# A new order for the end of the third block: high parts of the output projection's input in their own buffer, outputs and variances of the last heads ahead of the last gate tiles

## The reference, cut to what matters

```python
def _mixer_c(h, hg_s, lower_bound, w_in, hg_gn, w_out):
    qp, fp, ip, gp = _split(jnp.einsum('bld,de->ble', h, w_in), C_SPLITS)
    f = lower_bound + (1.0 - lower_bound) * jax.nn.sigmoid(fp)
    q, k, log_f, v = silu(qp), 1.0 - f, jnp.log(f), ip        # 8 heads of 128
    o, s_new = _hgrn2(q, k, log_f, v, hg_s)
    o = _head_norm(o, hg_gn, False) * jax.nn.silu(gp)         # per-head RMS norm, gain, gate
    return jnp.einsum('ble,ed->bld', o, w_out), s_new         # output projection
...
x = x + mix
h = _rmsnorm(x, p['ln_ffn'][l])
logits = h @ w_router + b_router; top-2 softmax; 8 experts of d_ff 2816; y = _rmsnorm(x + moe)
```

## Time and profile before

| | us |
|---|---|
| median of 3 runs | 1553.61 |
| lowest, highest | 1551.95, 1554.43 |
| the profiled execution, in all | 1554.71 |
| its span, first to last instruction | 1552.9 |
| TensorE busy | 1502.3 (97%) |
| VectorE busy | 1172.6 (76%) |
| ScalarE busy | 911.2 (59%) |
| GpSimd busy | 86.6 (6%) |
| HBM traffic over the span | 259 GB/s |

### The profile page before, as it was taken

How to read it: one execution, slowest core, us unless ns; L and a number is a source line. 1 busy time by engine, 2 the same in 40 slices (tenths; PEclk the granted TensorE clock), 3 DMA queues, 4 the chain that set the end, 5 groups by cost and what they waited for, 6 DMA issues and landing times.

```text
span 1552.9 us, 23238 instructions
## 1 busy us (share of the span) xinstructions
PE 1502.3 (97%) x8623; PEld 1326.7 (85%) x8623; DVE 1172.6 (76%) x1290; ACT 911.2 (59%) x907; POOL 86.6 (6%) x92
## 2 busy tenths in 40 slices
PE   7999998999999989998999999999999999999997
PEld 5899788999999989987878888888888888888885
DVE  5756677545456797666688898988989888898886
ACT  4544535443334553333477777868778787777863
POOL 1023100000000000111110000000000000000002
PEclk9999999999999999999999999999999999999999
DMA  8577624996456423433599999999999999999993
GB/s 215 155 135 149 115 86 119 287 295 196 129 149 194 139 72 98 136 119 94 199 400 348 392 366 400 388 357 385 369 392 394 365 384 359 399 378 379 392 356 118
DMA packets 214583, 403.86 MB, mean 260 GB/s; under 512 B 14467, under 2 KB 131503, under 8 KB 214386
## 3 DMA queue, kind: packets, MB, share of 16 engines
q1 hardware_dynamic: 203104, 372.82, 69.1%
q0 software_dynamic: 6208, 22.06, 4.6%
q10 hardware_dynamic: 5202, 8.03, 1.5%
HBM read 372.58 MB, written 30.28 MB: 259 GB/s over the span
## 4 chain that ended last, share of the span: by engine, by line
PE 88%; DVE 8%; issue 1%; ACT 1%; DMA 1%; DVEq 0%; ACTq 0%; SPq 0%
PE bank L485 26%; PE bank L486 25%; PE bank L487 25%; PE bank L688 2%; DVE dense_lo L1726 1%; PE bank L942 1%; PE bank L1089 1%; PE bank L730 1%; PE bank L625 1%; ACT dense_hi L1293 1%; DVE w_lo L2261 1%; PE bank L680 1%; DMA arena<-in_x_sample 1%; PE bank L643 0%; DVE arena L2098 0%
## 5 line engine op out<-in xcount | busy, mean ns | idle before, releaser
L2261 DVE TENSOR_TENSOR w_lo<-arena,w_hi 128x2048 fp32r<-128x2048 f32 (+1 forms) x280 | 597.0, 2165 | 86.3 <-ACT w_hi L1605 85.0
L1605 ACT ACTIVATE w_hi<-arena 128x2048 fp32r<-128x2048 f32 (+1 forms) x280 | 500.6, 1819 | 114.4 <-PE bank L487 112.6
L485 PE MATMUL bank<-w_hi,xg_hi 128*128 128x512 f32 (+1 forms) x768 | 288.1, 375 | 2.8 <-DVE w_lo L2261 2.3
L486 PE MATMUL bank<-w_lo,xg_hi 128*128 128x512 f32 (+1 forms) x768 | 286.7, 373 | 0.0
L487 PE MATMUL bank<-w_hi,xg_lo 128*128 128x512 f32 (+1 forms) x768 | 285.9, 372 | 0.0
L1726 DVE TENSOR_TENSOR dense_lo<-ring,dense_hi 128x2048 fp32r<-128x2048 f32 (+1 forms) x78 | 169.2, 2170 | 121.6 <-ACT dense_hi L1293 121.5
L1293 ACT ACTIVATE dense_hi<-ring 128x2048 fp32r<-128x2048 f32 (+1 forms) x78 | 140.5, 1803 | 160.2 <-PE bank L487 134.3
L485 PE MATMUL bank<-h_hi,dense_hi 128*128 128x320 f32 x512 | 165.6, 324 | 17.2 <-DVE h_lo_o L1738 6.2
L485 PEld LDWEIGHTS bank<-w_hi,xg_hi 128*128 128x128 f32 x768 | 144.9, 189 | 32.0 <-issue 3.5
L487 PEld LDWEIGHTS bank<-w_hi,xg_lo 128*128 128x128 f32 x768 | 144.6, 188 | 26.0
L486 PEld LDWEIGHTS bank<-w_lo,xg_hi 128*128 128x128 f32 x768 | 144.9, 189 | 25.0
(11 more groups left out here) (420 smaller groups left out, 2328.0 us busy)
## 6 DMA issues: line engine op xcount, KB each, us to landing
arena<-in_w_moe_down SPq DMA_DIRECT2D x176, 512.0 KB, 6.5
arena<-in_w_moe_gate SPq DMA_DIRECT2D x128, 512.0 KB, 6.7
arena<-in_w_moe_up SPq DMA_DIRECT2D x128, 512.0 KB, 6.7
arena<-in_w_moe_gate SPq DMA_DIRECT2D x64, 384.0 KB, 5.4
arena<-in_w_moe_up SPq DMA_DIRECT2D x64, 384.0 KB, 3.9
ring<-in_w_in_ab SPq DMA_DIRECT2D x32, 512.0 KB, 9.0
ring<-in_w_in_c SPq DMA_DIRECT2D x32, 512.0 KB, 4.6
expert_rows<-ZERO SPq DMA_DIRECT2D x12, 1024.0 KB, 7.6
```

The source lines that it names most:

```text
L485: mm(out, left[0], right[0], start=start, stop=False)
L486: mm(out, left[0], right[1], start=False, stop=False)
L1605: fn(WH[SLOT_OF[p]][:, 0:unit_size(p)], STAGE[:, s, 0:unit_size(p)], ACT.Copy).then_inc(S("unit_hi"), 1)
L2261: v.tensor_tensor(WL[w][:, 0:n], STAGE[:, s, 0:n], WH[w][:, 0:n].bitcast(F32), ALU.subtract).then_inc(S("unit_split"), 1)
```

## The change

The order behind g4 is rewritten. The outputs of heads 6 and 7, their squares and the second variance group now come before gate tile g7, and g6 after state5 and turn7; state4 comes before the first variance group. The high and low parts of the heads become steps of the list, "h u", on ScalarE and VectorE; the scales of heads 6 and 7 and the second root and reciprocal become ordinary steps too. The silu of the gates is taken in three calls, tiles 0 to 3, 4 and 5, 6 and 7. The high parts go to a buffer of their own, HH_O, at arena word 5120, where the squares lie, so that h u waits for the variance group of its head to be read. One memset moves from before `projected_out` to behind its additions. Number and kind of TensorE's matmuls, and all DMAs, are the same; ScalarE issues one silu call more.

```diff
--- before.py
+++ after.py
@@ -73,9 +73,9 @@
     xend0 kend0 v0 xb0 v1 pb0 wh db1 wh xb1 wl lb0 turn0 lb1 v2 la8 v3 db2 pb1 v4 wl wh xb2 wl out0 v5 v6 pb2
     lb2 db3 state0 turn1 v7 xb3 lb3 sq0 v8 wh pb3 out1 wl v9 turn2 db4 out2 sq1 db5 xb4 lb4 state1 v10 state2
     pb4 db6 xb5 g0 lb5 turn3 sq2 xb6 wh v11 pb5 out3 wh wl pb6 sq3 lb6 wl g1 db7 xb7 g2 pb7 g3 lb7 end1 state3
-    xend1 wh g4 lb8 kend1 g5 wh wl turn4 turn5 silug0 out4 wl sq4 gate0 out5 sq5 varc0 rootc0 state4 g6 gate1
-    gate2 mixc0 g7 gate3 state5 turn6 turn7 out6 mixc1 mixc2 mixc3 out7 state6 wl sq6 gate4 gate5 mixc4 sq7
-    gate6 mixc5 wh silug1 gate7 state7
+    xend1 wh g4 lb8 kend1 wh wl g5 turn4 turn5 silug0 out4 sq4 gate0 out5 sq5 wl gate1 state4 varc0 rootc0
+    turn6 gate2 gate3 state5 turn7 g6 out6 sq6 silug1 mixc0 mixc1 mixc2 mixc3 h0 h1 h2 h3 out7 sq7 gate4 gate5
+    mixc4 mixc5 h4 h5 varc1 rootc1 g7 state6 silug2 gate6 gate7 mixc6 h6 mixc7 h7 wh wl state7
 """.split()]
 
 CONST = {}
@@ -268,6 +268,7 @@
         HH = parts("h_hi", AT_HT, KD, NT)
         HL_A, HL_C, HL_O = parts("h_lo_a", AT_ARENA + 22064, KD, NT), parts("h_lo_c", AT_ARENA + 15616, KD, NT), \
             parts("h_lo_o", AT_ARENA + 20736, KD, NT)
+        HH_O = parts("h_hi_o", AT_ARENA + 5120, KD, NT)
         HH_F, HL_F = parts("h_hi_f", AT_ARENA + 15360, KD, NT), parts("h_lo_f", AT_ARENA + 17920, KD, NT)
         U_F, U_C = region(17920, KD, NT), region(15616, KD, NT)
 
@@ -853,11 +854,10 @@
                 w = need_unit(kind, 0, 0)
                 b = [open_bank("dve", j) for j in range(2)]
                 for n, k in enumerate(order):
-                    if k == HEADS[1][0]:
+                    if kind == "oab" and k == HEADS[1][0]:
                         for u in HEADS[1]:
                             head_scale(heads, u)
-                        if kind == "oab":
-                            n_rows()
+                        n_rows()
                     pe.wait_ge(S(out), n + 1)
                     for j in range(2):
                         ins = product3(b[j][:, 0:NT], [x[:, k, j * P:(j + 1) * P] for x in w], [x[:, k, :] for x in src],
@@ -991,8 +991,7 @@
                     after_empty(pe, (("V", 1, u // 4), u % 4 // 2, 2))
                     state_prompt(1, u)
                     piece_along(state_samples(1, u))
-            head_variances("hn1", 1)
-            projection_out("oc", (HH, HL_O), "hn1")
+            projection_out("oc", (HH_O, HL_O), "hn1")
 
 
             pe.wait_ge(S("router_in"), 32)
@@ -1414,7 +1413,8 @@
 
             def mixed_high(out, src, u):
 
-                fn(HH[:, u, :], src[:, u, :], ACT.Copy).then_inc(S(out + "_hi"), 1)
+                hi = {"mix0": HH, "mix1": HH_O}[out]
+                fn(hi[:, u, :], src[:, u, :], ACT.Copy).then_inc(S(out + "_hi"), 1)
 
             def centered(u):
                 b = take(("cen", u))
@@ -1553,8 +1553,8 @@
                     after_empty(act, ("c", "q", 7))
                     fn(Q[:, 4:8, :], Q[:, 4:8, :], ACT.Silu).then_inc(S("q_silu"), 1)
                 elif name == "silug":
-                    after_empty(act, ("c", "g", 4 * u + 3))
-                    at = slice(4 * u, 4 * u + 4)
+                    at = (slice(0, 4), slice(4, 6), slice(6, 8))[u]
+                    after_empty(act, ("c", "g", at.stop - 1))
                     fn(GC[:, at, :], GC[:, at, :], ACT.Silu).then_inc(S("g_silu"), 1)
                 elif name in ("xa", "xb"):
                     level_exps("ab".index(name[1]), 7 - u)
@@ -1574,14 +1574,12 @@
                     fn(SQH["hn1"][u], OH[:, u, :], ACT.Square).then_inc(S("hn1_squares"), 1)
                 elif name == "rootc":
                     head_roots("hn1", u)
+                elif name == "h":
+                    after_fill(act, ("hn1", "var", 0 if u in HEADS[0] else 1))
+                    after_empty(act, ("hn1", "scale", u))
+                    mixed_high("mix1", OH, u)
                 elif name == "state":
                     prompt_state(1, u)
-            after_fill(act, ("c", "g", 7))
-            for u in range(KD):
-                if u == 2:
-                    head_roots("hn1", 1)
-                after_empty(act, ("hn1", "scale", u))
-                mixed_high("mix1", OH, u)
             projected_out("oc", "n3")
             root("n3")
             b = take(("n3", "rt"))
@@ -1735,7 +1733,8 @@
             def mixed_low(out, src, u, lo, place):
 
                 dve.wait_ge(S(out + "_hi"), place + 1)
-                v.tensor_tensor(lo[:, u, :], src[:, u, :], HH[:, u, :].bitcast(F32), ALU.subtract).then_inc(
+                hi = {"mix0": HH, "mix1": HH_O}[out]
+                v.tensor_tensor(lo[:, u, :], src[:, u, :], hi[:, u, :].bitcast(F32), ALU.subtract).then_inc(
                     S(out + "_h"), 1)
 
             def gained(tag, row, k, dst):
@@ -2003,6 +2002,8 @@
                 if lo is not None:
                     low(tag, KD - 1, dst, lo, hi)
                     add_squares(tag, KD - 1)
+                else:
+                    v.memset(HN[SMP:P, 2, :], 0.0)
                 split_dense()
                 scale_of(tag)
 
@@ -2179,20 +2180,14 @@
                 elif name == "mixc":
                     dve.wait_ge(S("gated1"), u + 1)
                     scaled_head(OH, "hn1", u)
+                elif name == "h":
+                    mixed_low("mix1", OH, u, HL_O, u)
                 elif name == "gate":
                     dve.wait_ge(S("hn1_squares"), u + 1)
-                    dve.wait_ge(S("g_silu"), u // 4 + 1)
+                    dve.wait_ge(S("g_silu"), (1, 1, 1, 1, 2, 2, 3, 3)[u])
                     v.scalar_tensor_tensor(out=OH[:, u, :], in0=OH[:, u, :], scalar=prow("hg_gn", u), in1=GC[:, u, :],
                                            op0=ALU.mult, op1=ALU.mult).then_inc(S("gated1"), 1)
             after_fill(dve, ("lv", 1, 0))
-            for u in range(KD):
-                if u == 2:
-                    head_reciprocals("hn1", 1)
-                if u in HEADS[1]:
-                    dve.wait_ge(S("gated1"), u + 1)
-                    scaled_head(OH, "hn1", u)
-                mixed_low("mix1", OH, u, HL_O, u)
-            v.memset(HN[SMP:P, 2, :], 0.0)
             v.memset(ONE[SMP:P, 2, :], 0.0)
             projected_out("oc", "n3", 8, U_R)
             b = take("logit_rows")
```

## The result

The changed kernel takes 1544.46 us (median of 4 runs, 1543.50 to 1545.08), the kernel before beside it 1553.42 us (4 runs, 1551.95 to 1554.43). The ratio is 0.9944, 95% interval 0.9932 to 0.9956: 8.96 us less. The forecast was 1546.3, which is 7.3 us less than the runs known then.

A forecast was written before the change was run, and what follows sets the result against it. TensorE, 97% busy, was taken as the bound, with the experts hanging on the projection's last tile. Pure work 64.0, low clock 4.4 and waits 0.3 make 68.7 against 76.05 us: 7.3 less, 1546.3 us, range 1542.5 to 1551.5.

The forecast's parts named there:

- Rival 3: The experts' stage absorbs the earlier projection end, so the time stays at 1553.6 us; chance 0.08.
- The gaps, 6.16 us: TensorE's idle times before the output projection and its heads 6 and 7, 4.73 + 1.14 + 0.29 us, all to go.
- The layout by hand: Four engine queues laid out from 678.74 us by measured durations; projection to start at 717.2 instead of 722.02.
- The tight place at the second variances: Second variance group at 707.8 waits for head 7's square on ScalarE, ending at 707.6; 0.2 us spare.
- The other tight place: Third projection tile at 724.3 needs the second weight unit's low part, ending near 724.2; no spare to speak of.
- The table loads: An extra 1.28 us load on ScalarE from splitting the silu, without drain; with drains, some 2 us less gain.
- pure work: TensorE's time from g5's end to behind the projection without gaps or low clock, 64.0 us in both orders.
- the second episode: A second low-clock fall, likely between 703 and 709 us amid outputs, scales and variances without a weight tile: 1.5 us.
- the tight waits: Charge of 0.3 us for the two places with thin spare, bounded by 0 and 1.5 us.
- Rival 1: Third low-clock episode and both tight waits lost, 1.5 us each: gain 4.3 us, 1549.3 us; chance 0.16.
- Rival 4: Clock stays low from 684.6 until 3 us into the projection: 5.3 us slower, 1558.9 us; chance 0.09.
- Rival 2: The clock never falls in the new order: stretch 64.0 + 0.3, gain 11.7 us, 1541.9 us; chance 0.07.

The follow-up runs named there:

- e1: The kernel before, old order, with only the high parts moved to their own buffer HH_O and the memset moved: 1552.15 us, ratio 0.9994.
- e4: The changed kernel with gate tile g6 moved between the outputs of heads 4 and 5: 1544.98 us, ratio 0.9962 to the kernel before.
- e3: The changed kernel with one added TensorE wait before the projection, for the second weight unit's high part: 1551.06 us, ratio 1.0001 to the kernel before.
- e2: The changed kernel with the high parts back in the old shared buffer, so h0 to h5 stand behind g7: 1547.94 us, ratio 0.9968 to the kernel before.
- e6: The changed kernel with the silu of gate tiles 4 to 7 in one call behind g7 again: 1546.23 us, ratio 0.9964 to the kernel before.
- e7: The changed kernel with state4 and g6 between the outputs of heads 4 and 5, and state5 ahead of turn6: 1542.28 us, ratio 0.9921 to before.
- e9: The changed kernel with only state4 between the outputs of heads 4 and 5, and state5 ahead of turn6: 1541.58 us, ratio 0.9930 to before.
- e5: The changed kernel with state6 moved ahead of g7: 1546.34 us, ratio 0.9958 to the kernel before.
- a2: The changed kernel run again, unedited, in a second group on another chip: 1547.22 us, ratio 0.9968 to the kernel before.
- a3: The changed kernel run a third time, unedited, in a third group on another chip: 1545.34 us, ratio 0.9954 to the kernel before.
- e8: The kernel of e7 run again, unedited, on another chip: 1540.54 us, ratio 0.9927 to the kernel before.

## Why the prediction was right, and where it was off

**What bounds the kernel.** Right. TensorE's own gaps and clock set the stretch, and the end of the program moved with the router's product: 798.03 us behind it, 798.11 before, and 796.99, 797.02, 798.42 and 797.47 in e1 to e4, although their moments lie between 742.8 and 756.4. Rival 3, the shift not carried, is out. What is left of the spread goes with the clock behind the product: over all thirteen profiles it is 796.9 to 797.0 us where the clock never falls there, 797.5 to 798.7 with 6.8 us at 0.50 and 799.4 to 799.9 with 10.2. One reading of the earlier trace rows was too wide: the DMA engines are nearly free from 745 to 755, but their share is 1.09 in the slice from 684. Nothing in the forecast hung on it.

**The gaps, 6.16 us.** Right: all three are gone. e3 shows that they carried most of the gain, as a gap of 4.68 us put back brought 6.64 of the 9.73 us back on the stretch.

**The layout by hand.** It held to within 0.7 us against turn4, which starts 0.21 us later: scales from 701.61 (forecast 701.7), second variances at 707.69 (707.8), scale 6 at 714.08 (714.4), projection at 716.87 (717.2). The tight place at the second variances is visible on ScalarE. Its timeline after:

```profile
702.26 0.47 ACT L1574 ACTIVATE arena<-arena 128x320 f32<-128x320 f32 x1
702.75 1.28 ACT L1558 ACT_TABLE_LOAD   x1
704.04 0.74 ACT L1558 ACTIVATE arena<-arena 128x640 f32<-128x640 f32 x1
704.69 1.53 ACT L1417 ACTIVATE h_hi_o<-arena 128x320 fp32r<-128x320 f32 x4
...
707.08 0.47 ACT L1574 ACTIVATE arena<-arena 128x320 f32<-128x320 f32 x1
```

Head 7's square ends at 707.55 and the variances start at 707.69: 0.14 us spare where I had counted 0.2. The other tight place is VectorE's last split:

```profile
721.61 2.29 DVE L1724 TENSOR_TENSOR dense_lo<-ring,dense_hi 128x2048 fp32r<-128x2048 f32 x1 [1.31 <-ACT dense_hi L1292]
```

It ends at 723.90, and the third tile starts at 724.01 (forecast 724.2 and 724.3). Neither wait shows, so the 0.3 us that I charged were not due. Both are as thin as they were said to be: in e2 and e6, where this split comes later, the third tile waits 1.06 and 1.52 us, and in e6 the second variances wait 0.39. A third place was thinner than I had it. State 7's load was issued at 697.17 and not at 696.1; with the median 5.0 us to landing of this profile it lands near 703.1 (an estimate), and head 7's output starts at 703.85. I had counted 2.3 us of spare there, and e4 is where it runs out.

**The buffer.** I costed it at nothing and called it what lets h0 to h3 come before g7. Right on both, by e1 (0.9994) and e2 (2.2 us on the stretch).

**The table loads.** The load above starts 0.02 us behind the square and the silu follows it by 0.01 us. The Trainium skill, "ScalarE: Activation LUTs", What ACT_TABLE_LOAD costs, adds a drain of some 1.38 us to a switch; the trace shows none, and the 2 us that this would have cost did not come.

**The clock: the term that was mis-sized.** I put the low clock of before at 5.9 us lost and forecast 4.4 after, from two episodes. I had placed the starts of the falls by the spacing of the matmuls, at 684.6, 711.75 and 721.9. The slices of the earlier trace rows and these two of the kernel before put them at 684.2, 711.5 and 721.7:

```profile
711.00:712.00 1.00, 1.00 (x9) 0.57 (x6) 0.15 (x1) 0.64 (x2) 0.11 (x1) 0.75 0.15 46
...
721.00:722.00 1.00, 0.00 (x0) 0.01 (x1) 1.00 (x4) 0.35 (x1) 0.24 (x1) 0.87 0.15 51
```

The slices add up to 13.6 us at 0.50, of which 0.3 lie in the gap, so 6.7 were lost. With that the pure work is 63.2 us and not 64.0, as e7 to e9 measure it directly. After, one episode of 6.8 us cost 66.32 − 63.2 = 3.1. Four terms therefore moved: pure work 0.8 less, the second episode 1.5 less (it did not come), the first 0.2 more, and the tight waits 0.3 less. Together 68.7 became 66.3, and the gain on the stretch 9.7 instead of 7.3 us. The step that failed is "a second fall is likely between 703 and 709": I took the time since the last weight tile as the sign of a fall, and e5 has 11.5 us without one and no fall. With it went two of the signs that I had named, two episodes (there was one) and the router's product at 747 to 748 (745.27). The length of the one episode was luck: 3.4 us instead of 6.8, as in a2 and a3, would have made the stretch 64.7.

**The rivals.** Rival 1, a third episode and both tight waits lost, came in none of the three profiles of the changed kernel. Rival 4, the clock stays low, did not come; the longest episode of any profile was 10.2 us, not 25. Rival 2, the clock never falls, did not come for this order, and its reason was wrong even where its time is right. By the Trainium skill, "TensorE: Matmul & The Clock Gate", HAM oscillation, idle gaps bring the falls; e3 agrees (the fall lies inside the gap), while the fall at 684.8 in the changed kernel has no gap before it. It took another order of light work, e9, to reach a stretch without low clock, 63.2 us (rival 2 had 64.3).

**What is left open.** The first profile shows the longer episode (6.8 us) and its runs gave 0.9944, the repeats the shorter one (3.4 us) with 0.9968 and 0.9954. The differing low-clock time outside the stretch, 10 to 24 us ahead of it and 0 to 10.2 us behind it in the profiles, moves the runs by several us and hides 2 us effects; what sets it was not studied. The kernel before has only one profile of its own, so the 9.73 us on the stretch are one pair of executions. The version with the shortest stretch is e9, or e7: 1.5 to 3.1 us below the changed kernel, ratio 0.992 to 0.993 to the one before. In time that is not clear of the changed kernel beside it: the intervals of e8 and e9 overlap a3's, and e7's just touches a2's.

## What to carry to other kernels

Where one list sets every engine's queue, a gap on the bounding engine is often filled by moving independent light work of the other engines' queues ahead, not by a buffer: the buffer here was worth nothing alone and 2.2 us with the order. Price a gap together with the low clock that follows it, and lay the queues out by hand with the measured durations; here that gave the start of the projection within 0.4 us. Where executions differ by upstream clock, compare the same stretch of two traces and repeat the unchanged kernel in each group before crediting 2 us to an edit.

## What the runs showed of the hardware that was not expected

- TensorE's clock fell without any gap once the outputs of heads 4 and 5 (16 passes of 8 columns each) stood side by side or with only a weight tile between them, in each of ten such profiles, and there in none of the three profiles with a state product between them. The fall without a gap at 711.5 in the kernel before, behind the outputs of heads 6 and 7 with scales between them, did not come in e1 with the same order.
- The episodes lasted about 3.4, 6.8 or 10.2 us, and not always the same for the same instructions (3.4 twice and 6.8 once in the changed kernel). Matmuls cost about twice the time in them, so an episode costs half its length: 63.2, 64.7, 66.3 and 68.1 us for 0, 3.4, 6.8 and 10.2 us at the low level.
- Two switches of the activation table in a running queue of ScalarE (714.00 in the kernel before, 702.75 after) cost 1.28 us each and 0.01 to 0.02 us on either side.
